# An RWKV-7 layer in pairs of heads: one transpose for both banks of each updated inverse, with ScalarE's copy behind it, and preparation steps in other places

## The reference, cut to what matters

```python
def step(state, inp):
    r_t, w_t, k_t, v_t, a_t, b_t = inp
    sa = jnp.einsum('bhij,bhj->bhi', state, a_t)
    state = (state * w_t[:, :, None, :] + sa[..., None] * b_t[:, :, None, :]
             + v_t[..., None] * k_t[:, :, None, :])
    y_t = jnp.einsum('bhij,bhj->bhi', state, r_t)
    return state, y_t
...
w_log = -jax.nn.softplus(-(w0[direction] + jnp.tanh(xw @ w1[direction]) @ w2[direction])) - 0.5
decay = jnp.exp(-jnp.exp(heads(w_log).astype(jnp.float32)))
a = jax.nn.sigmoid(a0[direction] + (xa @ a1[direction]) @ a2[direction])
k_d = heads(k * (1.0 + (a - 1.0) * k_a)).astype(jnp.float32)
y = y + wkv7_scan(r_h, decay, k_d, v_h, -kk, kk * a_h, reverse=(direction == 1))
```

## Time and profile before

| | us |
|---|---|
| median of 3 runs | 1949.98 (1949.61 to 1953.52) |
| the profiled execution, its own time | 1954.62 |
| its span, first to last instruction | 1952.9 |
| start stage | 0 to 81 |
| the 8 pairs | 81 to 642 |
| of these a middle pair | 69.7 to 71.6 |
| the last pair | about 61 |

### The profile page before, as it was taken

How to read it: one execution, slowest core, us unless ns; L and a number is a source line. 1 busy time by engine, 2 the same in 40 slices (tenths; PEclk the granted TensorE clock), 3 DMA queues, 4 the chain that set the end, 5 groups by cost and what they waited for, 6 DMA issues and landing times. The chain is left out here.

```text
span 1952.9 us, 40263 instructions
## 1 busy us (share of the span) xinstructions
PE 1789.3 (92%) x17576; PEld 911.0 (47%) x17576; DVE 841.3 (43%) x1650; ACT 539.2 (28%) x1113; POOL 152.8 (8%) x230
## 2 busy tenths in 40 slices
PE   7889988988989959999999899999995999999988
PEld 4455555655656433333333346666543333333333
DVE  7766666667665242211222132777614211222122
ACT  3344355445343211111001112565510111010110
POOL 2101101101100210000000001112120000000000
...
DMA packets 92185, 459.69 MB, mean 235 GB/s; under 512 B 16998, under 2 KB 50155, under 8 KB 68203
## 3 DMA queue, kind: packets, MB, share of 16 engines
...
...
## 5 line engine op out<-in xcount | busy, mean ns | idle before, releaser
L1783 PE MATMUL banks<-arena 128*64 128x512 f32 x2944 | 654.8, 599 | 35.0 <-DMA arena<-in_moe_w_down 22.3
L1783 PEld LDWEIGHTS banks<-arena 128*64 128x64 f32 x2944 | 209.0, 137 | 443.7 <-issue 410.1
L547 PE MATMUL banks<-arena 128*128 128x512 f32 x384 | 198.9, 639 | 17.0 <-ACT arena L589 17.0
L1948 DVE TENSOR_TENSOR arena<-arena,banks 128x512 f32<-128x512 f32 x128 | 88.1, 688 | 284.0 <-PE banks L1805 284.0
L1888 ACT ACTIVATE arena<-banks 128x512 f32<-128x512 f32 x32 | 34.1, 1067 | 395.7 <-PE banks L1783 395.7
L855 PEld LDWEIGHTS banks<-arena 64*64 64x64 f32 x5120 | 96.4, 141 | 73.8 <-issue 49.4
L1932 DVE SCALAR_TENSOR_TENSOR arena<-arena,banks 128x512 f32<-128x512 f32 x32 | 34.0, 1063 | 219.4 <-ACT arena L1888 219.4
L855 PE MATMUL banks<-arena 64*64 64x64 f32 x5120 | 108.9, 229 | 12.8 <-DVE arena L1344 8.7
L1805 PE MATMUL banks<-arena 128*128 128x512 f32 x256 | 114.7, 598 | 1.5 <-DVE arena L1945 1.5
L1935 DVE SCALAR_TENSOR_TENSOR arena<-arena,small,banks 128x512 f32<-128x512 f32 x32 | 35.6, 1112 | 174.2 <-PE banks L1783 174.2
L547 PEld LDWEIGHTS banks<-arena 128*128 128x128 f32 x384 | 67.5, 195 | 76.6 <-issue 69.4
...
## 6 DMA issues: line engine op xcount, KB each, us to landing
...
```

Source lines behind the costliest of these rows:

```text
L547: last = nc.tensor.matmul(b[:, :], w_sl[:, n, k, :], xmix[n][:, k, :], start=(k == 0), stop=(k == ND - 1))
L1783: last = nc.tensor.matmul(b[z * CAP:(z + 1) * CAP, :], st[:, k, :], ring[g % RING][:, k, z * 512:(z + 1) * 512], start=(c % 2 == 0 and k = ...
L1948: nc.vector.tensor_tensor(xs, xs, b[:, :], ALU.add).then_inc(free[xj[("add", i, j)][0]], 1)
```

## The change

1. **Transposes and copies of the inverse.** Each updated inverse is transposed by one DVE instruction over both banks (2 x 256 columns). ACT waits for it (`turned_ready`) and then makes its three copies. `head_copied` and `head_turned` are gone.
2. **Level 0.** POOL writes the first blocks to a tile of their own, `first`, which lies where `xmix_g` lay, behind `ZM` and `states`. DVE transposes `first`; ACT moves the second head's half of it to the opposite partitions of `Um`, in four copies of 64x256, ahead of its tanh of w0; U of level 0 waits for them (`first_moved`). The X step of level 0 lands by `HEADS` like the others.
3. **Two tiles `tw` and two `ta`.** ACT's tanh of w1 and a1 no longer waits for `operands_ready`. The copy to `rk_cols` (L647) is gone.
4. **Order on DVE.** `("rate", 0)` stands at level 1, behind `("kn",)` and ahead of the transposes; its product with the normalised key is a piece of its own, `("iclr", d)`, and stays at level 2. The start stage has the same order.
5. **Order on ACT.** At level 0 `("k",)` stands ahead of `("cum", 0)`.
6. **Order on TensorE.** The two gate products (L1108, L1109 before) move from chunk step n = 3 of the chain to n = 1 and n = 2.

```diff
-        rT, kT, vT, kkn, kraw, tw, ta, cs, cx, rk_cols, e_neg = (body(S) for _ in range(11))
+        rT, kT, vT, kkn, kraw, cs, cx, rk_cols, e_neg = (body(S) for _ in range(9))
+        tw, ta = [body(S) for _ in range(2)], [body(S) for _ in range(2)]
...
+        first = [over(2, NT, CH) for _ in range(2)]
...
             if piece[0] == "wa":
                 d = piece[1]
-                if d == 1:
-
-                    act.wait_ge(operands_ready, 2 * u + 1)
-                else:
-                    act.wait_ge(cols_ready, u + 1)
-                for kind, dst, hc in (("w", tw, d), ("a", ta, 2 + d)):
+                act.wait_ge(cols_ready, u + 1)
+                for kind, dst, hc in (("w", tw[d], d), ("a", ta[d], 2 + d)):
...
-                nc.vector.tensor_scalar(tw, ta, -1.0, pc[:, V_KA:V_KA + 1], ALU.add, ALU.mult)
-                nc.vector.tensor_tensor(ta, ta, kkn, ALU.mult)
+                nc.vector.tensor_scalar(tw[d], ta[d], -1.0, pc[:, V_KA:V_KA + 1], ALU.add, ALU.mult)
                 dve.drain()
-                nc.vector.scalar_tensor_tensor(tw, tw, 1.0, kT, ALU.add, ALU.mult)
+                nc.vector.scalar_tensor_tensor(tw[d], tw[d], 1.0, kT, ALU.add, ALU.mult)
+                dve.drain()
+            if piece[0] == "iclr":
+                nc.vector.tensor_tensor(ta[d], ta[d], kkn, ALU.mult)
                 dve.drain()
...
             if piece[0] == "ops" and 2 in piece[2]:
-                if d == 0:
-                    nc.vector.tensor_copy(rk_cols, tw)
-                else:
-                    nc.vector.tensor_tensor(rk_cols, rk_cols, tw, ALU.add)
+                if d == 1:
+                    nc.vector.tensor_tensor(rk_cols, tw[0], tw[1], ALU.add)
...
-                        inverse_step(pe, ("X", lv, d, u), KEEP, inverse_at(lv), lambda q, h, m: LRB[d][q, h, m, 0, :],
+                        inverse_step(pe, ("X", lv, d, u), KEEP, HEADS, lambda q, h, m: LRB[d][q, h, m, 0, :],
...
-                        inverse_step(pe, ("U", lv, d, u), inverse_at(lv), KEEP if lv else HEADS, lambda q, h, m: Xm[d][q, h * NT + m, :],
-                                     lambda q, h, m: Um[d][q, h, m, :])
+                        if lv == 0:
+                            pe.wait_ge(first_moved, 2 * u + d + 1)
+                        inverse_step(pe, ("U", lv, d, u), HEADS, KEEP, lambda q, h, m: Xm[d][q, h * NT + m, :],
+                                     lambda q, h, m: (first if lv == 0 and h == 0 else Um)[d][q, h, m, :])
...
+                for d in range(2):
+                    act.wait_ge(blocks_ready, 2 * u + d + 1)
+                    for q in range(2):
+                        last = nc.scalar.copy(Um[d][half[1 - q], 1, :, :], first[d][half[q], 1, :, :])
+                    last.then_inc(first_moved, 1)
...
-                        last = nc.scalar.copy(own[:, 0, :], inverse[:, 0, :])
                         if lv < LAST:
-
-                            last.then_inc(head_copied[d], 1)
-                            act.wait_ge(head_turned[d], LAST * u + lv + 1)
-                        if lv == 0:
-                            last = nc.scalar.copy(own[:, 1, :], inverse[:, 1, :])
-                        else:
-                            for q in range(2):
-                                last = nc.scalar.copy(own[half[1 - q], 1, :], inverse[half[q], 1, :])
+                            act.wait_ge(turned_ready[d], LEVELS * u + lv + 2)
+                        nc.scalar.copy(own[:, 0, :], inverse[:, 0, :])
+                        for q in range(2):
+                            last = nc.scalar.copy(own[half[1 - q], 1, :], inverse[half[q], 1, :])
...
                     job_full(dve, rj, ("U", lv, d, u))
-                    inverse = two_banks(("U", lv, d, u))
-                    if lv:
-                        last = nc.vector.transpose(Tm[:, 1, d, :], inverse[:, 1, :])
-                    else:
-                        for q in range(2):
-                            last = nc.vector.transpose(Tm[half[1 - q], 1, d, :], inverse[half[q], 1, :])
-                    last.then_inc(head_turned[d], 1)
-                    dve.wait_ge(head_copied[d], LAST * u + lv + 1)
-                    nc.vector.transpose(Tm[:, 0, d, :], inverse[:, 0, :]).then_inc(turned_ready[d], 1)
+                    nc.vector.transpose(Tm[:, :, d, :], two_banks(("U", lv, d, u))).then_inc(turned_ready[d], 1)
```

49 lines of the change are left out of this document (27 added, 22 removed).

## The result

| | before | after |
|---|---|---|
| median | 1950.86 us (4 runs) | 1933.55 us (4 runs, 1930.85 to 1937.92) |
| profiled execution, its own time | 1954.62 | 1935.21 |
| span | 1952.9 | 1933.4 |
| the first states of the eight pairs reached at | 143.54, 215.10, 284.78, 355.43, 426.94, 498.22, 568.60, 630.95 | 134.73, 204.75, 276.45, 343.24, 411.48, 479.68, 549.32, 612.50 |

The ratio is 0.9912, with a 95% interval of 0.9888 to 0.9935. The kernel is faster, by 17.3 us on the medians and 19.4 us between the profiled executions. The forecast was 32.0 less than the profiled execution, a median of 1918, and 1908 to 1932 as a range. The time is outside it, on the slow side.

A forecast was written before the change was run, and what follows sets the result against it. The experts' saturated DMA stream follows the last pair, so gains in TensorE's waits move the end: 2.1 + 4.0 + 26.3 + 3.2 = 35.6, less 3.6 for the clock, 32.0; median 1918 us, range 1908 to 1932.

The forecast's parts named there:

- the replay: Pair 1's levels 1 to 4 re-timed after the change, counted from X1: PQ at 26.5 us against 30.7 before.
- with the same durations: Levels 1 to 4 in pair 1: times after the change come from replaying the earlier trace's operations at unchanged durations.
- The clock: TensorE in the pairs: falls in three pairs in seven at 1.2 us each, 3.6 us taken off the sum.
- Level 0: X steps on four quadrants free 0.9 us; 0.4 gained in pairs 1 to 6, 0.85 and 0.7 in pairs 0 and 7.
- The transposes: VectorE's one 128x512 transpose over both PSUM banks takes 0.72 us, bounds 0.70 and 0.90.
- Levels 1 to 4: From X1 to PQ: pair 1 gains 4.2 us, six pairs 3.3 each, pair 0 6.4; 26.3 in all.
- The chain: Gate products moved behind the first two states cover TensorE's 0.46 us wait there; 3.2 us over 7 pairs.
- The start stage: Rate operations fill VectorE's idle time ahead of the key's normalisation, and copy L647 goes: 2.1 us gained.
- The last pair: It prepares nothing, so only level 0 is counted there: 0.7 us gained.
- The median: The profiled execution stood 4.6 us above the median, so 1922.6 for it becomes a median of 1918.
- Rival 3: The clock falls once in every pair, seven falls at 1.7 us: 1926 us; chance 0.18.
- Rival 4: ScalarE becomes the bound, its copies delaying X2, x0, w1 and X4 by 0.5 us each: 1932 us; chance 0.06.

The follow-up runs named there:

- e1: The kernel after with the r load (and wo's in pair 6) issued behind the chain's first gate product: 1925.98 us, ratio 0.9871.
- e4: The kernel after with the old exchange of banks (two half transposes, copies side by side) instead of one transpose over both: 1934.92 us, ratio 0.9903.
- e12: e4 with the loads of r and wo moved as in e1: 1933.57 us, ratio 0.9906.
- e8: e7 with r copied by VectorE, y's scaling in the chain, and w1's tanh between ScalarE's two copies of U3: 1905.16 us, ratio 0.9763.
- e9: The kernel before with two tiles tw and ta, direction 0's rates at level 1, `iclr` apart, k ahead of ScalarE's exponentials: 1939.83 us, ratio 0.9932.
- e10: e9 with the loads of r and wo moved as in e1: 1938.37 us, ratio 0.9928.
- e7: e1 with w0's tanh ahead of level 0's four moves and VectorE's rates behind level 1's transposes: 1915.57 us, ratio 0.9811.

## Why the prediction was wrong, point by point

I add up four things for each kernel, from the first pair's start to the last pair's first state: TensorE's stalls for instructions, all its other waits in the list, half of the time at 1.2 GHz (the most that it can cost), and what remains.

| | length | issue | other waits | at 1.2 GHz | length less issue, waits and half of that |
|---|---|---|---|---|---|
| before | 549.6 | 3.3 | 47.4 | 43.3 | 477.2 |
| after | 532.8 | 8.3 | 41.0 | 22.2 | 472.4 |
| e1 | 523.5 | 3.3 | 42.8 | 8.7 | 473.0 |
| e4 | 533.7 | 8.6 | 36.3 | 25.2 | 476.2 |
| e12 | 530.1 | 3.7 | 39.9 | 20.5 | 476.3 |
| e8 | 500.6 | 4.5 | 19.8 | 6.8 | 473.0 |
| e9 | 539.7 | 8.8 | 34.8 | 30.7 | 480.8 |
| e10 | 532.4 | 3.8 | 38.1 | 12.5 | 484.3 |

The last column moves by 0.6 us between after and e1 and by 0.1 between e4 and e12, which differ in the loads alone, but by 3.5 between e9 and e10. So the sum is complete to about a microsecond for the first six rows, and not for every kernel. Each row is one execution. From before to after it reads: instructions +5.0, other waits -6.4, clock -10.6, the rest (the faster X0 above all) -4.8; together -16.8. The clock's part is an upper bound: of the 43.3 us TensorE sits idle in 4.6, of the 22.2 in 0.6, and without these it is 8.6.

By stretches, the profiled execution missed the forecast by 12.5 us: 6.9 from X1 to PQ in the six middle pairs (169.5 us, against six times the replay's 26.5 and the 3.6 for the clock), 2.4 behind PQ up to the first state, 1.9 at their level 0, 0.5 up to the first pair's first state, 2.0 in the last pair, less 1.1 behind the pairs and 0.1 of rounding and the chain.

- **The step that failed: "with the same durations".** The replay moved TensorE's work forward as if its instructions were always there. No term, bound or rival had their supply in it, though the page of the profile has a queue for it, and the waits of before had 2.6 us of "issue" in two places, which I left aside as small. The sum named for each wait what is late next among engines, and not what had been late under the wait all along. This is 5.0 us more than before directly. The replay had none of it: 7.4 us of stalls stand from X1 to PQ in the six middle pairs (2.6 before), and part of them is covered again by the waits behind them. Not all of the miss is this step; the rest is the clock and level 0, below.
- **The clock.** I took 3.6 us for it out of "three pairs in seven at 1.2 us each". The number of falls was right, their size was not: pairs 1, 2 and 6 of the first seven have one, with 13.7 us at 1.2 GHz, which cost up to 6.8. In all there are 22.2 us in five falls, where before had 43.3; the other two are one ahead of the first pair, at 78 us as before, and one in the last pair. Two of the five, those at 187 and 535 us, begin 0.2 and 1.3 us after the end of the stalls of pairs 1 and 6, and e1 has neither; it has 8.7 us at 1.2 GHz in all. In e1, then, the stalls give back 5.0 us and the clock up to 6.7, of which the other waits take 1.8 again. Its profiled execution stands 29.0 us below that of before, which is the forecast's 32.0 but for 3; by the medians, which the forecast was for, it is 25 us (ratio 0.9871), so 7 are lacking. TensorE: Matmul & The Clock Gate of the Trainium skill (Why this matters for your kernels) has only longer waits bring the clock down. Most of the trace agrees: with nearly no stalls, six of e1's eight pairs have no fall. But the one at 327 us in e1 comes behind waits of at most 1.2 us (x0 1.17, v0 0.70, U4 1.07), as the one at 267 us did before, and in pair 2 of e1 no fall comes with a wait of 1.97 us, where one comes with the same wait in the kernel after (at 262.3). So the length of a single wait doesn't decide it.
- **Level 0: right in kind.** X0 takes 1.3 us with the four quadrants (2.08 before), the four moves on ScalarE 1.66 us as one group, against 1.5 from the copies of the earlier trace rows, and k0 then waits 0.68 us. From X0 to X1 a middle pair takes 10.29 us against 10.37, so the change gains 0.1 there, and I had said 0.4. e7, which puts the tanh first, has 9.58.
- **The transposes: right.** The estimate was 0.72 for 128x512 from PSUM, from the earlier trace rows; the 64 of them took

```profile
L1312 DVE STREAM_TRANSPOSE arena<-banks x64: 672/716/718, 96.5 to 598.1; 128x512 f32<-128x512 f32 x64
```

- **Levels 1 to 4: right**, to 0.1 us at each of nine places, in pair 3, the one middle pair without a stall. Pair 0, which has none either, takes 23.96 us from X1 to PQ, 23.9 in the replay, and pairs 4 to 6 of e1 take 26.4 to 26.7.
- **The chain: right.** 3.7 us in 8 waits against 6.9 in 15; the forecast was 3.2 less.
- **The start stage: 1.7 us**, for 2.1 forecast. The first pair starts at 79.71 instead of 81.37, and the normalised key at 62.88 has no wait in front of it any more, against the earlier trace rows.
- **The last pair: a sign wrong.** From first state to first state it takes 63.2 us against 62.4. From X0 to X1 it takes 11.29 us, 10.20 before, where 0.7 of gain was counted: X0 waits 1.74 us for the transpose of the blocks (1.30 before), and the clock falls right behind, at 573 us. In e1, where it doesn't fall there, this stretch takes 9.64. Then X4 waits 0.62 us for ScalarE's copies, and 0.54 is a stall; neither was counted. The chain of pair 6, which lies in this stretch too, gives 1.0 back.
- **The median.** The profiled execution of before stood 4.6 us above its median, that of after 1.7 above. So 2 to 3 us of what was read off the profile were a difference of two executions and not of two kernels: 19.4 us between the profiles, 17.3 between the medians. The mean granted clock of the profiled execution of before, 0.970, is at the low end of that kernel's runs (0.968 to 0.976), so it probably had more slow matmuls to lose than a usual one.
- **The rivals.** Rival 3, the clock falling in every pair, gave 1926, nearer than the forecast, but it didn't happen: the clock fell in four of the eight pairs, and the stalls, which no rival had, came on top. Rival 4 (ScalarE as the bound) is refuted by the timeline of pair 3. PSUM — Partial Sum Buffer of the Trainium skill (Specifications (TRN2)), on both engines reading PSUM at once, spoke for the exchange, and e1 against e12 decides for this kernel: the exchange is 7 us slower, not faster. No run here tests the page itself. The reason isn't that TensorE waits longer in sum. U4's mask is 1.5 us later with the exchange, but X2 and x0 wait less, and the other waits of e12 are 2.9 us below those of e1. What stands against it in the table is the clock, up to 5.9 us, and 3.3 in the last column: in e12 the clock falls in pairs 3 to 6, each time within 1 us of the end of U4's wait of 2.5 us, and in e1 once, in pair 3.

What stays open: why pair 2's stall is left (1.33 to 1.76 us in e1, e7, e8, e10 and e12), with no r load in the way of its packet. That packet starts 1.8 to 2.5 us after TensorE passes the previous border, in these kernels and in the kernels before and after alike (2.5 and 2.4), where pair 3 of e1 has 0.6; so the r load isn't what makes it late in the kernel after either. Open is also how much of the clock's share comes from the stalls and how much from the other short waits, as no run here separates them in each pair.
